# Walking a product's moving operand from both halves in turn, in a Strassen-like fp32r trunk

## The reference, cut to what matters

```
hn = rms_norm(x, norm1_g)
z = gelu(hn @ w_in)                      # 1024x1024 @ 1024x4096
u, v = split(z, 2)
v = layer_norm(v) * ln_g                 # then by 128-position chunks and 8 groups:
sv = tril(w_s[g]) @ v[chunk, g] + b_s    # a 128x128 product per chunk and group
x = x + (u * sv) @ w_out                 # 1024x2048 @ 2048x1024
h = rms_norm(x, norm2_g)
x = x + square(relu(h @ w1)) @ w2        # 1024x1024 @ 1024x4096, 1024x4096 @ 4096x1024
out = rms_norm(x, final_g)
```

## Time and profile before

| | |
|---|---|
| median of 3 runs | 1123.69 us (1122.48 to 1124.07) |
| the profiled execution, its own time | 1122.82 us |
| its span in the trace | 1121.1 us |
| TensorE busy | 1109.7 us (99%) |
| VectorE busy | 797.3 us (71%) |
| ScalarE busy | 563.8 us (50%) |
| granted TensorE clock | 0.999 of full |

### The profile page before, as it was taken

One profiled execution on the slowest core, in us unless ns is written; L12 is line 12 of the kernel. 1 busy time (PEld: TensorE's weight loads), 2 busy tenths in 40 slices (PEclk: granted clock), 3 DMA queues, 4 the chain that ended last, 5 costly groups with the idle time before them and its releaser, 6 DMA issues.

```text
span 1121.1 us, 13119 instructions
## 1 busy us (share of the span) xinstructions
PE 1109.7 (99%) x5050; PEld 922.0 (82%) x5050; DVE 797.3 (71%) x878; ACT 563.8 (50%) x873; POOL 23.0 (2%) x17
## 2 busy tenths in 40 slices
PE   9999999999999999999999999999999999999997
PEld 7888888888888888887788888888888888888886
DVE  5885656689779986699858447465598575777756
ACT  7764344554554334644674455454643343333455
POOL 0000000000000000000000000000000000000340
PEclk9999999999999999999999999999999999999999
DMA  9072353272875594643353535527877354343213
GB/s 336 21 219 101 116 179 105 101 252 83 310 265 187 193 350 153 186 122 104 113 188 150 188 112 205 194 105 276 294 295 290 128 204 188 113 153 111 84 66 151
DMA packets 86543, 195.91 MB, mean 175 GB/s; under 512 B 5048, under 2 KB 15312, under 8 KB 79824
## 3 DMA queue, kind: packets, MB, share of 16 engines
q1 hardware_dynamic: 85168, 194.28, 49.3%
q10 hardware_dynamic: 1312, 0.79, 0.3%
HBM read 134.23 MB, written 58.72 MB: 172 GB/s over the span
## 4 chain that ended last, share of the span: by engine, by line
PE 91%; DVE 4%; ACT 2%; issue 1%; DMA 1%; ACTq 0%; SPq 0%; DVEq 0%
PE banks L438 29%; PE banks L443 29%; PE banks L442 29%; PE banks L531 3%; DVE left_and_right L1465 1%; DVE ring_low L1429 1%; DMA left_and_right<-in_a_w_in_dram 1%; ACT ring_high L990 1%; ACTq L396 0%; DVE rows L1571 0%; ACT raw_a L1039 0%; DVE raw_a L1525 0%; DVE raw_s L1398 0%; DVE s_low L1515 0%; DVE s_low L1510 0%
## 5 line engine op out<-in xcount | busy, mean ns | idle before, releaser
L1020 ACT ACTIVATE pair_high<-left_and_right 128x1024 fp32r<-128x1024 f32 x168 | 177.2, 1060 | 247.5 <-PE banks L438 199.9
L1429 DVE TENSOR_TENSOR ring_low<-left_and_right,ring_high 128x512 fp32r<-128x512 f32 x224 | 152.7, 691 | 185.4 <-ACT ring_high L990 184.6
L1437 DVE TENSOR_TENSOR pair_low<-left_and_right,pair_high 128x1024 fp32r<-128x1024 f32 x168 | 204.1, 1229 | 109.1 <-ACT pair_high L1020 109.0
L990 ACT ACTIVATE ring_high<-left_and_right 128x512 fp32r<-128x512 f32 x224 | 137.9, 628 | 253.4 <-PE banks L438 155.5
L438 PE MATMUL banks<-pair_high 128*128 128x512 f32 x672 | 261.7, 389 | 0.0
L443 PE MATMUL banks<-pair_high,pair_low 128*128 128x512 f32 x672 | 261.5, 389 | 0.0
L442 PE MATMUL banks<-pair_low,pair_high 128*128 128x512 f32 x672 | 261.4, 389 | 0.0
L438 PE MATMUL banks<-s_high,ring_high 128*128 128x512 f32 x384 | 149.9, 390 | 2.0 <-DVE s_low L1510 1.4
L442 PE MATMUL banks<-s_low,ring_high 128*128 128x512 f32 x384 | 149.4, 389 | 0.0
L443 PE MATMUL banks<-s_high,ring_low 128*128 128x512 f32 x384 | 149.4, 389 | 0.0
L443 PEld LDWEIGHTS banks<-pair_high,pair_low 128*128 128x128 f32 x672 | 126.1, 188 | 26.3
(11 more groups left out here) (129 smaller groups left out, 1217.3 us busy)
## 6 DMA issues: line engine op xcount, KB each, us to landing
left_and_right<-sums SPq DMA_DIRECT2D x40, 1024.0 KB, 6.9
left_and_right<-in_mlp_w_dram SPq DMA_DIRECT2D x36, 1024.0 KB, 7.5
sums<-rows SPq DMA_DIRECT2D x34, 1024.0 KB, 5.3
left_and_right<-in_a_w_in_dram SPq DMA_DIRECT2D x19, 1024.0 KB, 7.3
v_blocks<-rows SPq DMA_DIRECT2D x8, 1024.0 KB, 4.5
left_and_right<-in_a_w_out_dram SPq DMA_DIRECT2D x8, 1024.0 KB, 10.0
rows<-in_x_dram SPq DMA_DIRECT2D x7, 1024.0 KB, 9.3
spare<-v_blocks SPq DMA_DIRECT2D x6, 1024.0 KB, 6.7
```

The lines of the kernel that those rows point to most:

```text
L990: nc.scalar.activation(ring_high[k][:, :], right_place(n, pos)[:, k, :], ACT.Copy)\
L1020: nc.scalar.activation(pair_high[pair_entry(d, pos, k)][:, :, :], pair_of(d, pos, k), ACT.Copy)\
L1429: nc.vector.tensor_tensor(ring_low[k][:, :], right_place(n, pos)[:, k, :], ring_high[k][:, :].bitcast(F32), ALU.subtract).then_inc(low_don ...
L1437: nc.vector.tensor_tensor(pair_low[e][:, :, :], pair_of(d, pos, k), pair_high[e][:, :, :].bitcast(F32), ALU.subtract).then_inc(low_done, 1)
```

## The change

The moving operand of every large product is read in another order. `walked` turns the run of 512 columns into a pattern that takes column 0 of the first half, column 0 of the second, column 1 of the first, and so on. The stationary operands are read as before, and the bank is written in a run as before, so that its word 2i + h now holds column 256h + i. What empties a bank undoes this: `result` reads the bank as two passes with a step of two words, and `halves` describes the tile in `rows` as two runs of 256, so that everything in `rows` lies as before. Where `activate` reads `rows` and not a bank, source and destination are both described as two runs. The products of `mini`, the transposes and what reads their banks are left alone. The instructions of every engine, their order and their waits are the same as before; only the patterns of operands differ.

```diff
+        def walked(mov):
+
+            return mov.rearrange("p (h i) -> p i h", h=2)
+
+        def halves(row):
+
+            return row.rearrange("p (h i) -> p h i", h=2)
+
+        def result(bank):
+
+            return ps[:, bank, :].rearrange("p (i h) -> p h i", h=2)
...
             def products(bank, stat_high, stat_low, mov_high, mov_low, start, stop, begins):
+                mov_high, mov_low = walked(mov_high), walked(mov_low)
                 first = nc.tensor.matmul(ps[:, bank, :], stat_high, mov_high, start=start, stop=False,
                                          skip_group_check=True)
...
-                    mm = nc.tensor.matmul(ps[:, banks[m], :], rows_high[:, c], ring_high[0][:, :], start=True,
+                    mm = nc.tensor.matmul(ps[:, banks[m], :], rows_high[:, c], walked(ring_high[0][:, :]), start=True,
...
-                    nc.scalar.activation(block_of[blk][:, m, :], ps[:, banks[m], :], ACT.Copy)\
+                    nc.scalar.activation(halves(block_of[blk][:, m, :]), result(banks[m]), ACT.Copy)\
                       .then_inc(drained[banks[m]], 1)
...
                 if blk == "c21":
                     filled(act, ("product", n, pos), bank)
-                    return ps[:, bank, :]
+                    return result(bank)
                 emptied(act, ("product", n, pos), bank)
-                return block_of[blk][:, m, :]
+                return halves(block_of[blk][:, m, :])
...
-                    nc.scalar.activation(block_of[blk][:, m, :], src, ACT.Relu)\
+                    nc.scalar.activation(halves(block_of[blk][:, m, :]), src, ACT.Relu)\
                       .then_inc(drained[banks[m]] if blk == "c21" else relued, 1)
...
-                    nc.vector.tensor_tensor(block_of["c21"][:, m, :], ps[:, bank, :], scale_b[:, 1, :], ALU.mult)\
+                    nc.vector.tensor_tensor(halves(block_of["c21"][:, m, :]), result(bank), halves(scale_b[:, 1, :]),
+                                            ALU.mult)\
                       .then_inc(drained[bank], 1)
...
-                    nc.vector.tensor_tensor(block_of[blk][:, m, :], ps[:, bank, :], block_of[blk][:, m, :], ALU.add)\
+                    nc.vector.tensor_tensor(halves(block_of[blk][:, m, :]), result(bank),
+                                            halves(block_of[blk][:, m, :]), ALU.add)\
                       .then_inc(drained[bank], 1)
...
-                    piece = block_of[blk][:, m, :]
+                    piece = halves(block_of[blk][:, m, :])
                     if d == 0:
-                        nc.vector.tensor_tensor(piece, ps[:, bank, :], piece, ALU.add).then_inc(drained[bank], 1)
+                        nc.vector.tensor_tensor(piece, result(bank), piece, ALU.add).then_inc(drained[bank], 1)
                     else:
                         nc.vector.scalar_tensor_tensor(
-                            out=piece, in0=ps[:, bank, :], scalar=y_r2[:, 4 * tb + m:4 * tb + m + 1], in1=piece,
+                            out=piece, in0=result(bank), scalar=y_r2[:, 4 * tb + m:4 * tb + m + 1], in1=piece,
                             op0=ALU.mult, op1=ALU.add).then_inc(drained[bank], 1)
```

More of the change, by code:

```diff
@@ L486, in first_unit @@
                     c = slice(m * P, (m + 1) * P)
-                    nc.tensor.matmul(ps[:, banks[m], :], rows_low[:, c], ring_high[0][:, :], start=False,
+                    nc.tensor.matmul(ps[:, banks[m], :], rows_low[:, c], walked(ring_high[0][:, :]), start=False,
                                      stop=False, skip_group_check=True)
@@ L491, in first_unit @@
                     c = slice(m * P, (m + 1) * P)
-                    nc.tensor.matmul(ps[:, banks[m], :], rows_high[:, c], ring_low[0][:, :], start=False,
+                    nc.tensor.matmul(ps[:, banks[m], :], rows_high[:, c], walked(ring_low[0][:, :]), start=False,
                                      stop=False, skip_group_check=True)
@@ L1129, in activate @@
                         t = 4 * (int(blk[1]) - 1) + m
-                        nc.scalar.activation(block_of[blk][:, m, :], src, ACT.Gelu_apprx_tanh, scale=x_rstd[:, t:t + 1])\
+                        nc.scalar.activation(halves(block_of[blk][:, m, :]), src, ACT.Gelu_apprx_tanh, scale=x_rstd[:, t:t + 1])\
                           .then_inc(drained[banks[m]] if blk == "c21" else acted, 1)
```

## The result

The changed kernel takes 1086.0 us in the median of four runs (1085.3 to 1086.7), against 1123.8 before in the runs beside it. The ratio is 0.967, with a 95% interval from 0.965 to 0.968: 37.8 us less. The forecast was no change; the case that came is the first rival, the walk that removes the surplus, at about three fifths of its full size.

A forecast was written before the change was run, and what follows sets the result against it. TensorE's 4704 products at 226.7 ns were taken as the bound. The profiled 1122.8 us plus 0 for the moving read and 0 for bank reads gave no change, forecast as the median 1123.7 us; range 1063 to 2130 us.

The forecast's parts named there:

- the first rival: Every large product: the new read order removes the 13.3 ns beyond 512 column times; 1061 to 1063 us, chance 0.29.
- the surplus: Every large product: 13.3 ns, or 32 column times, beyond the 213.3 ns of 512 columns; 62.7 us over 4704 products.
- What bounds the kernel: TensorE, busy 1109.7 of 1121.1 us: 4704 products at 226.7 ns each, 1066 us, explain most of the span.
- the price of the moving read: Alternating moving read in every product on TensorE: taken as zero, assuming two places are held at a time.
- the half rate: Rival, every product: a column only every second cycle, +1003 us, 2127 us; chance 0.27 for 1879 to 2127.
- a fixed cost at each change of stationary operand: Argument against the fast case: such a cost between products would look the same as 13.3 ns lost in sequential reading.
- The bounds of that term: Moving read: at most 62.7 us gained; lost, +755 us by VectorE's transpose ratio 1.75 or +3405 by its time per element.
- The trace's stepped row: VectorE's transpose L1525, step of four words: 1083 ns for 512 elements against 680 contiguous, 1.75 times per element.
- The bank reads at nothing: 188 VectorE and 120 ScalarE stepped bank reads: taken as free; at the upper end 403 ns each, hidden under TensorE.
- the tight stretch: 350 to 400 us, VectorE busy 49.29 of 50: up to 4.1 us late if bank reads slow; 2.2 given back if products quicken.
- the pace and nowhere else: Sign of failure: whether the moving read fails to hold two places or gains by it shows only in product start spacing.
- The rule on lines of 16 bytes: Skill note on SBUF reads: two successive hits per line needed for full rate; taken literally every column pays, about 2127 us.

The follow-up runs named there:

- the run without the step: Changed kernel with VectorE's sixteen transposes reading four blocks in a run instead of with a step of four words: 1077.5 us, ratio 0.9593.
- The table of forms above: Small separate kernel, rows of 36 like products per read order: sequential 226.7 ns a product, alternating from two places 215.8, step of two words 451.
- near4: Form in the small separate kernels: moving read alternates within blocks of 2 x 4 columns instead of in sequence; 215.8 ns a product against 226.7 at 512 columns.

## Why the prediction was wrong

**What bounds the kernel** held: 4704 products at their pace, and a pace that moved by 10.8 ns a product, 51 us in all, moved the span by 36.3.

**The step that failed is the price of the moving read, "I take zero".** It measured -10.8 ns a product. Of the two questions behind it the first was answered rightly: two places are held, and the half rate didn't come. The second was left as a rival at 0.29, against 0.31 for no change: whether the 32 column times of surplus belong to the sequence. They do, all but 6 of them (2.5 ns). The forecast saw the surplus in the rows, found that a stationary load is too short to be its cause, and then treated its persistence as the likeliest without a row that said so. What it set against the rival, a fixed cost at each change of stationary operand, is refuted by the same operand each time (227.8 ns). The bounds of that term were right at the lower end (62.7 us; 51.0 measured) and empty at the upper: neither the ratio nor the time of the stepped transpose carried over to TensorE's walk. The trace's stepped row said something true of a step (step of four words on TensorE: 460 ns, 2.03 times 226.7; of the transpose: 1057 ns against 676 in a run), and nothing of two interleaved runs. That the range, 1063 to 2130 us, holds 1086 is no merit of the sum: it was wide enough for the fast rival and the half rate together.

**The bank reads at nothing** was right: 679 and 743 ns on VectorE and 597 on ScalarE, against 680, 743 and 596, and the other half of the change alone left the time at a ratio of 0.9999.

**The rival that came** put 62.7 us down for the whole surplus and 2.2 back from the tight stretch at 350 to 400 us. The gain was 51.0 us, and the loss 13.2 by the medians (51.0 - 37.8), or 15 by the spans, most of it from 450 to 550 us and none from 350 to 400, where TensorE was busy for 50.00 us of 50. So the rival had the gain right and the place and size of the loss wrong, for two reasons. The stretch from 500 to 550 us had 46.11 us of VectorE in 50 before the change, less than the 49.29 at 350, but TensorE already waited in it (2.0 us); the busy share alone doesn't tell that. And an unchanged instruction got slower, which the forecast, with its signs in "the pace and nowhere else", had no place for: of the 13.2 us, 4.6 are the slowing of the transposes (1085.6 less 1081.0 with the same pace), and 3.5 more go when the step is gone too (1081.0 to 1077.5; these two kernels also differ in their walk). The remaining 5 or so weren't taken apart. Part of them shows in the timeline of the run without the step: near 57 us a product starts 1.35 us behind the one before it, after a wait on ScalarE, where the kernel before had 0.65, and at 810 and 813 us two start 0.86 us behind, after waits on `pair_low`, where it had no gap.

**The rule on lines of 16 bytes** (the Trainium skill, "SBUF — State Buffer", "Door 1: The DMA port swizzle") gave the half rate for this change, and the measurement decides against it in this form: 215.8 ns. The table of forms above bears the rule out where each line serves a single column in turn (a step of four words, 460 ns) and contradicts it at a step of two fp32 words, two hits to a line, which it lets pass and which took 451. What its "Vector Engine (DVE) Microarchitecture Reference" tells under "Measured stream behaviour on trn2", of a read stream of VectorE that alternates between two regions at full rate, was the better guide to TensorE's walk.

## What to carry to other kernels

If a kernel is bound by fp32r products of many columns, let the moving operand alternate column by column between two runs of at least four words: 215.8 ns in place of 226.7 for 512 columns, provided that what empties the bank can undo it in a pattern that costs nothing, as a step of two words did here. Don't do it for bf16 (472 ns for 216), don't alternate in longer pieces or over more places, and keep the start of the runs and the stationary operand as they are here: three kinds of offset and a stepped stationary operand each took the gain back. Prefer neighbouring runs of four to distant halves where other engines read SBUF with a step. When a sum holds a surplus that no row explains, and the change touches what the surplus may hang on, don't take it as fixed: a small kernel with both forms side by side settles it. And after a bound has moved, look for the stretch in which the bounding engine already waits, not for the one with the highest busy share elsewhere.

## What the runs showed of the hardware that was not expected

VectorE's stepped SBUF read depends on how TensorE reads meanwhile: 512 elements with a step of four words took VectorE 1044 to 1078 ns under sequential products, 1522 under a walk over places 256, 320 or 512 words apart, and 1049 to 1102 under equally quick walks over 4, 260, 264, 268, 272, 288, 516 or 1020 words. Reads in a run took 676 to 686 ns under sequential products, under the walk from halves and under near4; the other distances weren't tried on them. And a sequential fp32r read is not TensorE's quickest: at 32 stationary columns it lost 4.2, 8.6 and 15.9 ns at 128, 256 and 512 columns against the alternating one.
